# The samples' GDN states are read in two halves, one ahead of the GLA states and one behind them

## What is computed

```python
def gla_recurrent(q, k, v, log_a, s0):
    def step(s, inp):
        qt, kt, vt, at = inp
        s = jnp.exp(at)[..., None] * s + kt[..., None] * vt[..., None, :]
        return s, jnp.einsum('bhd,bhde->bhe', qt, s)
...
def gdn_recurrent(q, k, v, g, beta, s0):
    def step(s, inp):
        qt, kt, vt, gt, bt = inp
        s = jnp.exp(gt)[..., None, None] * s
        u = bt[..., None] * (vt - jnp.einsum('bhd,bhde->bhe', kt, s))
        s = s + kt[..., None] * u[..., None, :]
        return s, jnp.einsum('bhd,bhde->bhe', qt, s)
```

## Time and profile before

| | |
|---|---|
| profiled execution, time | 1854.26 us |
| its span, first to last instruction | 1851.9 us |
| median of three runs | 1855.71 us |
| PE busy | 1814.0 us (98%) |
| VectorE (DVE) busy | 1150.0 us (62%) |
| ScalarE (ACT) busy | 796.2 us (43%) |
| GpSimd (POOL) busy | 183.2 us (10%) |
| granted TensorE clock, mean | 0.998 |
| DMA, mean over the span | 198 GB/s |

### The profile page before, as it was taken

The page is one execution under the profiler, slowest core; times in us unless marked ns, Lnnn a source line. Parts: engine busy times, 40 slices in busy tenths (PEclk is TensorE's granted clock), DMA queues, the critical chain, the costliest instruction groups (busy, mean ns, idle before and its releaser), DMA issues.

```text
span 1851.9 us, 34219 instructions
## 1 busy us (share of the span) xinstructions
PE 1814.0 (98%) x13818; PEld 1723.1 (93%) x13818; DVE 1150.0 (62%) x1573; ACT 796.2 (43%) x842; POOL 183.2 (10%) x185
## 2 busy tenths in 40 slices
PE   8999999999999999999999999999999999999997
PEld 6999999988999999888749999999999999999997
DVE  6888447746766577555676656666544566665443
ACT  6454545343363533443642344443333444443344
POOL 5000000002106300000005500000000000000231
PEclk9999999999999999999999999999999999999999
DMA  8555554472045667797784688886456899984553
GB/s 266 162 166 174 180 167 155 137 241 76 17 154 177 216 211 247 276 311 250 251 283 128 190 239 249 250 249 193 129 183 193 239 249 248 249 225 134 170 187 110
DMA packets 415128, 367.19 MB, mean 198 GB/s; under 512 B 11519, under 2 KB 374014, under 8 KB 414486
## 3 DMA queue, kind: packets, MB, share of 16 engines
q1 hardware_dynamic: 387368, 340.76, 60.0%
q10 hardware_dynamic: 27678, 25.26, 4.2%
HBM read 347.84 MB, written 18.35 MB: 198 GB/s over the span
## 4 chain that ended last, share of the span: by engine, by line
PE 89%; DVE 5%; ACT 2%; issue 1%; POOL 1%; DMA 1%; DVEq 0%; ACTq 0%; POOLq 0%
PE ps L467 65%; PE ps L543 9%; PE ps L524 4%; DVE w_lo L446 2%; PE ps L961 1%; PE ps L510 1%; PE ps L1245 1%; ACT w_hi L439 1%; PE ps L1260 1%; PE ps L1163 1%; PE ps L1084 1%; PE ps L1402 1%; DMA gst<-in_state_gla_dram 1%; PE ps L1448 1%; PE ps L1440 1%
## 5 line engine op out<-in xcount | busy, mean ns | idle before, releaser
L439 ACT ACTIVATE w_hi<-raw 128x2048 fp32r<-128x2048 f32 (+1 forms) x285 | 512.3, 1797 | 857.6 <-PE ps L467 709.9
L446 DVE TENSOR_TENSOR w_lo<-raw,w_hi 128x2048 fp32r<-128x2048 f32 (+1 forms) x285 | 620.1, 2176 | 261.3 <-ACT w_hi L439 258.1
L467 PE MATMUL ps<-act_hi,w_lo 128*128 128x264 f32 x2560 | 732.8, 286 | 6.2 <-DVE w_lo L446 4.1
L467 PE MATMUL ps<-act_lo,w_hi 128*128 128x264 f32 x2560 | 725.4, 283 | 0.0
L467 PE MATMUL ps<-act_hi,w_hi 128*128 128x264 f32 x2560 | 724.9, 283 | 0.0
L467 PEld LDWEIGHTS ps<-act_hi,w_lo 128*128 128x128 f32 x2560 | 482.2, 188 | 10.6 <-issue 3.9
L467 PEld LDWEIGHTS ps<-act_lo,w_hi 128*128 128x128 f32 x2560 | 482.5, 188 | 0.4
L467 PEld LDWEIGHTS ps<-act_hi,w_hi 128*128 128x128 f32 x2560 | 480.0, 187 | 0.0
L467 PE MATMUL ps<-ff_hi,w_lo 128*128 128x264 f32 x704 | 201.1, 286 | 0.0
L467 PE MATMUL ps<-ff_hi,w_hi 128*128 128x264 f32 x704 | 200.1, 284 | 0.0
L467 PE MATMUL ps<-ff_lo,w_hi 128*128 128x264 f32 x704 | 199.4, 283 | 0.0
(11 more groups left out here) (444 smaller groups left out, 2172.9 us busy)
## 6 DMA issues: line engine op xcount, KB each, us to landing
raw<-in_w_in_dram SPq DMA_DIRECT2D x56, 1024.0 KB, 7.5
raw<-in_ffn_w_gate_dram SPq DMA_DIRECT2D x44, 1024.0 KB, 5.7
raw<-in_ffn_w_up_dram SPq DMA_DIRECT2D x44, 1024.0 KB, 5.7
raw<-in_ffn_w_down_dram SPq DMA_DIRECT2D x32, 768.0 KB, 4.8
raw<-in_ffn_w_down_dram SPq DMA_DIRECT2D x32, 640.0 KB, 6.1
raw<-in_w_out_dram SPq DMA_DIRECT2D x16, 1024.0 KB, 6.3
raw<-in_xa_w_q_dram SPq DMA_DIRECT2D x16, 1024.0 KB, 6.7
raw<-in_xa_w_k_dram SPq DMA_DIRECT2D x16, 1024.0 KB, 6.3
```

The source lines that it names most:

```text
L439: act.activation(w_part(ph, w_hi[b]), raw_part(ph, r, half), ACT.Copy)\
L446: dve.tensor_tensor(w_part(ph, w_lo[b]), raw_part(ph, r, half), w_part(ph, w_hi[b]), ALU.subtract)\
L467: mm = pe.matmul(ps[:, acc(ph, u), 0:ph.cols], w[b][:, k, :], v[:, kk + k, 0:ph.cols], start=first and k == 0 and m == 0, stop=last and k ...
```

## The change

SP reads state_gdn in two transfers of 4 samples each, by a new local function `state_half(m)`. Half 0 is issued where the whole was; half 1 is issued behind the two halves of gst, ahead of the save, the prompt's state and the restore of x. Both count on `bst_landed`, so PE waits for 32 and not 16 ahead of on_state(0). Bytes, row length and what is computed stay as they are.

```diff
@@ -732,11 +732,17 @@
             stream("z")
 
             sp.wait_ge(lo_split, PH["w_out"].u0 + LO_CREDIT)
-            sp.dma_start(bst[:, :, :, :], a["state_gdn"][0].rearrange("b h k v -> k b h v")).then_inc(N["bst_landed"], 16)
+            def state_half(m):
+
+                sp.dma_start(bst[:, 4 * m:4 * m + 4, :, :], a["state_gdn"][0][4 * m:4 * m + 4].rearrange("b h k v -> k b h v"))\
+                  .then_inc(N["bst_landed"], 16)
+
+            state_half(0)
             sp.wait_ge(units_done, PH["w_out"].u0 + UNIT_CREDIT)
             for m, landed in enumerate((N["sstate_landed"], second_half_landed)):
                 sp.dma_start(gst[:, 4 * m:4 * m + 4, :, :], a["state_gla"][0][4 * m:4 * m + 4].rearrange("b h k v -> k b h v"))\
                   .then_inc(landed, 16)
+            state_half(1)
 
             W(sp, "gla_tok", 8)
             sp.dma_start(new_rows[0:NB, :], gvrow[:, :]).then_inc(new_rows_kept, 16)
@@ -1200,7 +1206,7 @@
                 mm = turn(ps[:, 5, 256 + e * 32:256 + (e + 1) * 32], grow[:, e * P:(e + 1) * P])
             mm.then_inc(N["gla_turned"], 1)
             pe.wait_ge(columns_ready, 2)
-            pe.wait_ge(N["bst_landed"], 16)
+            pe.wait_ge(N["bst_landed"], 16 * 2)
             on_state(0)
             on_state(1)
             pe.wait_ge(gla_done, 1)
```

## The result

The changed kernel takes 1858.15 us in the median of 20 runs (1855.85 to 1860.45), the kernel before 1855.36 us (20 runs, 1853.64 to 1857.95): ratio 1.0015, 95% interval [1.0009, 1.0021]. That is 2.8 us slower, within the 0.2% of "no change" but clear of noise. The execution that was profiled took 1860.45 us (span 1858.6), 2.3 us over its own median; why is part of the story.

The account below looks back on a forecast made before the run. The tensor engine, busy 98% of the span, was taken as the bound. Change is the larger of -1.88 and (save landed - 412.87): +2.5 us on the median 1855.71 gives 1858.2 us, range 1853.8 to 1861.0.

Parts of the forecast that it names:

- The 1.88 us wait goes: Tensor engine's wait before the first GLA-state products: first GLA half lands at 400.9 to 402.4, ahead of 403.48; 1.88 us gained.
- The dry queue makes the save late: SyncE's queue runs dry for 4.3 us before the GLA halves; the 32 KB save lands at 415.4, not 411.42.
- Where the stall goes: Tensor engine's third group of transposes waits for ScalarE's ktok copy: start 416.05 against 413.52, +2.5 us.
- The clock: Rival 1: the clock falls in the 4.4 us stall, +2.5 and about +2.0, together +4.5 us, 1860.2; chance 0.28.
- the bounds of 1.4 to 2.5: Cost in us of returning to full clock after the stall: 1.4 from the start's slow products, plus at most doubled transposes.
- the base: Median of the runs shown for the kernel before, 1855.71 us, on which the forecast of 1858.2 was put.
- the likeliest case: The forecast itself: stall at the third group of transposes, +2.5 us, 1858.2 us; chance 0.46.
- the longest pause of the middle: Tensor engine's 2.00 us idle stretch ahead of 503.94, taken as the middle's longest, with the granted clock left at 1.00.
- The save passing the big read: Rival 3: in SyncE's queue the save lands by 411.0, the whole 1.88 us is kept, 1853.8 us; chance 0.11.
- The landing tied to the return of the issue: Rival 2: the save lands 6.0 us after its issue returns, at 413.3 to 414.4; +0.4 to +1.5, 1856.7; chance 0.12.
- Cover: Second GDN half lands by 415.7, wanted at 425.89 less the gain; the last two groups and pairs, over 8 us, cover it.

Follow-up runs that it names:

- The three cuts: The changed kernel with six, four (the change itself) or two samples' GDN states read ahead of the GLA states: 1854.18, 1858.15 and 1862.85 us.
- the pauses filled: Changed kernel with idle products in the stall and two later pauses, 1855.83 us, against the kernel before with the two later pauses filled, 1853.63 us.
- the second (1859.07 - 1855.48 - 2.2): The changed kernel unaltered, timed again beside the run with the filled stall: 1859.07 us against 1855.48 for the kernel before.
- the cut alone: Changed kernel with both GDN halves issued where the whole read stood, ahead of the GLA states: 1855.30 us against 1855.43 for the kernel before.

## Why the prediction was right, point by point

- **The 1.88 us wait goes.** It went. The GLA halves moved from about 393.5 (forecast 394.0), and the first landed at 400.2, earlier than either bound (400.9 to 402.4).
- **The dry queue makes the save late.** Forecast dry from 389.7 to 394.0, ktok released at 415.4 (414.1 to 415.7); measured dry from 389.6 to about 393.5, released at 415.05. Reading the landing off the row of the same transfer was 0.35 us too late, because the queue restarted sooner after the issue. The three cuts show the cause and its size.
- **Where the stall goes.** Forecast third group at 416.05 and +2.5 us; measured 415.70 and +2.18 in the profile, +2.20 with the pauses filled. The term was 0.3 us too large.
- **The clock.** Forecast as a rival of 0.28 with +2.0 us on top. It is not a case beside the others but a part of the distribution, and the clock was lower in all three traces with an unfilled stall of 4 us or more. It cost 2.9, 1.6 and 1.6 us: twice inside the bounds of 1.4 to 2.5, once over them. The kernel before has falls of its own, so less shows in the medians: the measured loss is 0.6 us over the stall's 2.2 in the first measurement and 1.4 in the second (1859.07 - 1855.48 - 2.2). That the median forecast, 1858.2, meets 1858.15 so closely is luck, since three errors cancel: the base was 0.35 us too high (1855.71 from three runs, 1855.36 from twenty), the stall 0.3 us too dear, and the likeliest case had no clock, which was worth 0.6.
- **A wrong reading.** The text says the longest pause of the middle is 2.00 us and that it left the clock at 1.00. The engine's waits have one of 2.40 us ahead of 455.75 as well, and both pauses can bring the clock down, as the trace of the cut alone shows; the profiled execution of before happened to keep it. The conclusion, that a longer stall may lose the clock, was right; its premise, that the present pauses are harmless, was not: they cost the kernel before 1.7 us in the median.
- **The rivals.** The save passing the big read (faster) did not happen: it was seen 0.2 to 0.3 us behind the landing ahead of it in the kernel before (411.42 after 411.2) and in the change (415.05 after 414.8). The landing tied to the return of the issue did not hold either: 6.0 us after it before, 4.1 us after it now (410.98 to 415.05). Within the three cuts it is 4.1 us each time, so they alone would not tell this rival from the forecast; what speaks against it is the 6.0 us of before. The Trainium skill's page "DMA: Bandwidth & Descriptors", section "Queues, rings and completion order", has each ring consumed in order; both traces agree, with the 0.2 to 0.3 us.
- **Cover.** The second GDN half landed at 414.8, 16 us ahead of its use, and the longer hold of SyncE's issues (10.64 us for the save) reached nobody else.

## What to carry to other kernels

When transfers in a queue are reordered, price everything that stands behind them, the small ones too. The save here had the same bytes ahead of it as before; it was only later. Those 32 KB, with 1.45 us of slack and on the bytes of a tile that the critical engine waits for, cost more than the reordering gained. A piece that is small enough to end before the next issue is allowed leaves the queue dry, and everything behind is late by that gap. And give a small save either its place ahead of the bulk or bytes of its own; both got the gain back.

## What the runs showed of the hardware

- TensorE's granted clock can fall to 0.50 after a pause of only 2.0 to 2.4 us, in some executions and not in others of the same program. It can fall inside the pause (at 414.9 in the 4.07 us stall) or after work has begun again (1.2 us after the 2.00 us pause), and the same stall lost it at 414.9 in one execution and at 415.8 in another. Each fall in the later pauses costs 1.6 to 1.9 us (steps at 1851.8, 1853.4 and 1855.3), those in the stall 1.6 to 2.9 us.
- Filling pauses with products of no use brings an even time: 1853.47 to 1853.87 instead of 1853.53 to 1857.27.
- One fp32 product of 128x128 by 128 columns is two instructions and 0.22 us at full clock; counting products in the code and timing instructions in the trace is off by two.
- Reads in rows of 512 B ran at about 290 GB/s and in rows of 1 KB at about 350, in the changed kernel as in the one before.
